# Three other sequences of matmuls for the first feed-forward weight, one per segment

## The reference

```
h = rmsnorm(x, g_mlp[l])
u = jnp.square(jax.nn.relu(jnp.einsum('bsd,df->bsf', h, w_ff1[l])))     # 2048 -> 8192
x = x + jnp.einsum('bsf,fd->bsd', u, w_ff2[l])                          # 8192 -> 2048
```

## Time and profile before

| | |
|---|---|
| median of 3 runs | 2403.76 us (2403.4 to 2403.99) |
| the profiled execution | 2401.66 us, of which the span from first to last instruction is 2399.9 us |
| PE busy | 2392.3 us (100%), 12653 matmuls |
| PEld busy | 2048.4 us (85%), 12653 weight loads |
| DVE busy | 1515.0 us (63%) |
| ACT busy | 1168.0 us (49%) |
| DMA | 452.13 MB, mean 188 GB/s, queue 1 at 58.7% |
| granted TensorE clock | 1.00 over the whole span |

### The profile page before, as it was taken

One profiled execution on the slowest core, in us unless ns is written; L12 is line 12 of the kernel. 1 busy time (PEld: TensorE's weight loads), 2 busy tenths in 40 slices (PEclk: granted clock), 3 DMA queues, 4 the chain that ended last, 5 costly groups with the idle time before them and its releaser, 6 DMA issues.

```text
span 2399.9 us, 30366 instructions
## 1 busy us (share of the span) xinstructions
PE 2392.3 (100%) x12653; PEld 2048.4 (85%) x12653; DVE 1515.0 (63%) x1536; ACT 1168.0 (49%) x1353; POOL 0.2 (0%) x4
## 2 busy tenths in 40 slices
PE   9999999999999999999999999999999999999999
PEld 8788888888888888888888888888888888888887
DVE  6575656666566466566556667855777577756774
ACT  5454454455444344344344555555555455535552
POOL 0000000000000000000000000000000000000000
PEclk9999999999999999999999999999999999999999
DMA  7556556565556665665655565555565665566564
GB/s 251 160 178 197 165 189 196 193 188 197 186 177 203 194 220 193 194 191 190 194 188 182 188 186 164 167 183 185 185 185 196 189 192 177 202 193 187 181 208 143
DMA packets 238037, 452.13 MB, mean 188 GB/s; under 512 B 16569, under 2 KB 20779, under 8 KB 237771
## 3 DMA queue, kind: packets, MB, share of 16 engines
q1 hardware_dynamic: 237147, 449.07, 58.7%
q10 hardware_dynamic: 752, 1.12, 0.1%
HBM read 446.46 MB, written 3.67 MB: 188 GB/s over the span
## 4 chain that ended last, share of the span: by engine, by line
PE 99%; DVE 1%; ACT 0%; DMA 0%; issue 0%; ACTq 0%; DVEq 0%
PE PS L71 99%; DVE WL L71 0%; DMA VR<-in_g_mix 0%; DVE PB L71 0%; DVE TA L71 0%; ACT TA L71 0%; ACT WH L71 0%; DVE SEL L71 0%; DVE NC L71 0%; ACT XHL L71 0%; DVE XHL L71 0%; DVE XT L71 0%; DVE CR L71 0%; DVE SQ L71 0%; ACT CR L71 0%
## 5 line engine op out<-in xcount | busy, mean ns | idle before, releaser
L71 DVE TENSOR_TENSOR WL<-RAW,WH 128x1024 fp32r<-128x1024 f32 (+1 forms) x844 | 1021.9, 1221 | 745.9 <-ACT WH L71 745.6
L71 ACT ACTIVATE WH<-RAW 128x1024 fp32r<-128x1024 f32 (+1 forms) x845 | 881.6, 1054 | 901.7 <-PE PS L71 885.9
L71 PE MATMUL PS<-XHL,WH 128*128 128x512 f32 x3984 | 1252.9, 396 | 1.8 <-DVE CR L71 1.3
L71 PEld LDWEIGHTS PS<-XHL,WL 128*128 128x128 f32 x3968 | 745.4, 188 | 176.1
L71 PE MATMUL PS<-XHL,WL 128*128 128x256 f32 x3968 | 779.6, 278 | 0.0
L71 PE MATMUL PS<-WH,MHL 128*128 128x512 f32 x2240 | 694.1, 390 | 0.0
L71 PEld LDWEIGHTS PS<-XHL,WH 128*128 128x128 f32 x3984 | 606.5, 188 | 6.1 <-DVE CR L71 1.5
L71 PEld LDWEIGHTS PS<-WH,MHL 128*128 128x128 f32 x2240 | 420.4, 188 | 87.1
L71 PE MATMUL PS<-WL,MHL 128*128 128x512 f32 x1120 | 435.8, 389 | 0.0
L71 PEld LDWEIGHTS PS<-WL,MHL 128*128 128x128 f32 x1120 | 210.3, 188 | 42.9
L71 DVE TENSOR_TENSOR TA<-TA,PS 128x1024 f32<-128x1024 f32 x72 | 87.9, 1221 | 9.0 <-ACT TA L71 1.8
(11 more groups left out here) (129 smaller groups left out, 785.9 us busy)
## 6 DMA issues: line engine op xcount, KB each, us to landing
RAW<-in_w_ff SPq DMA_DIRECT2D x256, 512.0 KB, 3.7
RAW<-in_w_in SPq DMA_DIRECT2D x224, 512.0 KB, 3.9
RAW<-in_w_up SPq DMA_DIRECT2D x176, 512.0 KB, 4.0
RAW<-in_w_down SPq DMA_DIRECT2D x88, 512.0 KB, 4.3
RAW<-in_w_mix_out SPq DMA_DIRECT2D x32, 512.0 KB, 3.9
RAW<-in_w_out SPq DMA_DIRECT2D x32, 512.0 KB, 3.7
RAW<-in_w_conv_out SPq DMA_DIRECT2D x16, 512.0 KB, 3.7
RAW<-in_w_attn_out SPq DMA_DIRECT2D x16, 512.0 KB, 4.4
```

Of the source, the lines that this page charges most:

```text
L71: ins = step[1](*step[2], **step[3])
```

## The change

Each segment of w_ff1 is given a name for its sequence: "bank" for segment 0, "short" for segment 1, "one" for segment 2, "two" for segment 3. "two" is the sequence of before, and stays for all other feature items.

- "bank": within a unit, bank by bank: h of both chunks, l of both chunks, then the next bank. The shapes are the same, and so is their order by shape (h, h, l, l); what differs is which bank and which weight block each goes to.
- "one": for each chunk and bank h and then l.
- "short": no matmul of 512 columns. For each chunk and bank three of 256 columns, all onto columns 0:256 of the bank: WH against the high piece, WH against the low piece, WL against the high piece. The bank's right half isn't used, so `fold` becomes a single copy by ACT.

In all feature items, those that keep "two" as well, the waits for both chunks of a unit now stand ahead of the unit's first matmul, where each chunk's wait stood ahead of that chunk's matmuls.

```diff
+FF1_ORDER = ("bank", "short", "one", "two")
...
-                for k, kc in enumerate(kcs):
+                for kc in kcs:
                     PE.wait([need(kc, tok)])
-                    st = first and k == 0
-                    en = last and k == len(kcs) - 1
-                    for j0 in range(0, len(banks), 2):
-                        two = list(enumerate(banks))[j0:j0 + 2]
-                        for j, bank in two:
-                            PE.do(mm, PS[:, b + bank, :], h[:, k, j * P:(j + 1) * P], src[:, kc, :],
-                                  start=st, stop=False, inc=False)
-                        for j, bank in two:
-                            end = j == len(banks) - 1 and k == len(kcs) - 1
-                            t = PE.do(mm, PS[:, b + bank, 0:T], l[:, k, j * P:(j + 1) * P], src[:, kc, 0:T],
-                                      start=False, stop=en, inc=end)
+                nb, nk = len(banks), len(kcs)
+                if order == "two":
+                    work = [(k, j, w, 0, m) for k in range(nk) for j0 in range(0, nb, 2)
+                            for w, m in (("h", 2 * T), ("l", T)) for j in range(j0, min(j0 + 2, nb))]
+                elif order == "bank":
+                    work = [(k, j, w, 0, m) for j in range(nb) for w, m in (("h", 2 * T), ("l", T)) for k in range(nk)]
+                elif order == "one":
+                    work = [(k, j, w, 0, m) for k in range(nk) for j in range(nb) for w, m in (("h", 2 * T), ("l", T))]
+                else:
+                    work = [(k, j, w, c, T) for k in range(nk) for j in range(nb)
+                            for w, c in (("h", 0), ("h", T), ("l", 0))]
+                begun = set()
+                for i, (k, j, w, c, m) in enumerate(work):
+                    start = first and j not in begun
+                    begun.add(j)
+                    stop = last and all(x[1] != j for x in work[i + 1:])
+                    t = PE.do(mm, PS[:, b + banks[j], 0:m], (h if w == "h" else l)[:, k, j * P:(j + 1) * P],
+                              src[:, kcs[k], c:c + m], start=start, stop=stop, inc=i == len(work) - 1)
...
-            a = A.step(nc.scalar.copy, TA[:], PS[:, b:b + 4, T:2 * T], after=[t, evac_done[0]])
-            v = V.step(tt, TA[:], TA[:], PS[:, b:b + 4, 0:T], add, after=[a])
+            if whole:
+                v = A.step(nc.scalar.copy, TA[:], PS[:, b:b + 4, 0:T], after=[t, evac_done[0]])
+            else:
+                a = A.step(nc.scalar.copy, TA[:], PS[:, b:b + 4, T:2 * T], after=[t, evac_done[0]])
+                v = V.step(tt, TA[:], TA[:], PS[:, b:b + 4, 0:T], add, after=[a])
```

More of the change, by code:

```diff
@@ L334, in take, with feature_item @@
             return s, b
-        def feature_item(parts, src, tok, mid=(), small=False, ahead=AHEAD):
+        def feature_item(parts, src, tok, mid=(), small=False, ahead=AHEAD, order="two"):
             s, b = side() if small else take()
@@ L365, in feature_item @@
                 flush()
-            return s, b, t
+            return (s, b, t, True) if order == "short" else (s, b, t)
         def f_item():
@@ L423, in token_item, with fold @@
             return s, b, done if tail else t
-        def fold(s, b, t):
-            a = A.step(nc.scalar.copy, TA[:], PS[:, b:b + 4, T:2 * T], after=[t, evac_done[0]])
-            v = V.step(tt, TA[:], TA[:], PS[:, b:b + 4, 0:T], add, after=[a])
+        def fold(s, b, t, whole=False):
+            if whole:
[3 more added lines that the diff above has]
+                v = V.step(tt, TA[:], TA[:], PS[:, b:b + 4, 0:T], add, after=[a])
             free[s] = [v]
@@ L987, in build @@
                 mid = {2: [lambda: turn_x_item(3, G_MLP, xtok)], 4: [lambda: norm_columns("r2", "sum")]} if seg == 0 and g == 0 else {}
-                it = feature_item(wide(io["w_ff1"][0], 0, ALLK, 2048 * seg + 512 * g), XHL, xtok, mid)
+                it = feature_item(wide(io["w_ff1"][0], 0, ALLK, 2048 * seg + 512 * g), XHL, xtok, mid,
+                                  order=FF1_ORDER[seg])
                 later(ff_evac(it, g, "r2", utok, seg == 0 and g == 0))
```

## The result

| | before | after |
|---|---|---|
| median of 20 runs each | 2402.38 us (2401.71 to 2403.99) | 2406.80 us (2406.51 to 2408.36) |
| ratio after to before | | 1.0019, 95% interval 1.0012 to 1.0026 |
| span of the profiled execution | 2399.9 us | 2405.0 us |
| matmuls | 12653 | 12909 |

What follows compares the result with a forecast made beforehand. PE, busy throughout, was taken as the bound, so time sums distances between matmul starts. Terms 3.0 + 0 + 0 + 0.4 = +3.4 us gave 2405.1 us profiled, 2407.2 us for the median; 8-in-10 range 2402.0 to 2411.5 us.

Steps and rivals of the forecast that it cites:

- "short", +3.0 us: w_ff1 segment 1: 120 ns per short matmul, a triple of 360 ns, 11.7 more than a pair, 256 times.
- The first reading: Segment 1: fixed 16.5 ns per matmul plus 0.411 ns a column, same in both item kinds; triple 364.8 ns, +4.2 us.
- The second reading: Segment 1: h costs f_item's 231.7 ns, leaving l 116.6 ns; triple 349.8 ns, +0.4 us.
- "one", 0: w_ff1 segment 2: same 256 h and 256 l as before, alternating, so no change in time.
- Rival 2: Segments 0 to 2: each successor in the same bank costs 5.0 ns more; +9.2 us in all, 2413.0 us; chance 0.13.
- "bank", 0: w_ff1 segment 0: same 256 h and 256 l, shapes following each other as before, so no change in time.
- Loads keep up: Segment 1: weight loads recorded with 188 ns overlap, transposes' loads stand 109 ns apart, so one every 120 ns fits.
- Fold and units' splitting, 0: Segment 1: DVE loses four additions of 1.22 us off the chain; ACT's copies and idle room leave PE unaffected: 0.
- Hoisted wait, +0.4 us: Program's first unit: PE waits for both chunks' low pieces before its first matmul, +0.4 us, once.
- Rival 1: Segment 1: cost goes by columns, not matmuls; triple 345 to 350 ns, whole change -0.4 to +0.8 us; chance 0.24.
- rival 4: Segment 1: weight loads too slow for an unbroken run of short matmuls; +55 us, 2459 us; chance 0.03.
- Rival 3: Pace at an item's start kept in "bank" and "one", triple 345 ns: -2.2 us, 2401.6 us; chance 0.10.

Runs made afterwards that it cites:

- tensors: Changed kernel with w_ff1 segment 2 alternating weights WH and WL, 512 columns for both: segment 116.06 us, 453.4 ns a pair.
- lag: Changed kernel with w_ff1 segment 1 alternating h and l, each l following the h of another bank and weight block: 90.23 us, 352.5 ns a pair.
- hoist_only: Changed kernel with all four w_ff1 segments back in sequence "two", hoisted waits kept: ratio to before 1.0001 (0.9992 to 1.0010).
- sizes: Changed kernel with w_ff1 segment 0 alternating 512 and 256 columns, both with weights from WH: segment 90.22 us.
- short_only: Changed kernel with only segment 1 in "short", the other segments in "two", hoisted waits kept: ratio to before 1.0012 (1.0003 to 1.0021).
- entry_two: Kernel before, with each feature item's first unit in "two" and its seven others in "one", waits as before: ratio 0.9985, median 2398.42 against 2402.11 us.
- all_one: Kernel before, with every feature item in "one", waits as before: ratio 1.0035 (1.0023 to 1.0048), median 2411.14 against 2403.45 us.
- entry_mid: As entry_two, with the unit behind small matmuls queued in the middle of an item also in "two": ratio to before 0.9984 (0.9975 to 0.9993).
- lead_unit: Every unit of every feature item starts h, h, l, l over two banks, then alternates h, l: ratio to before 1.0022 (1.0013 to 1.0031).

## Why the prediction was right, and where it wasn't

The forecast was 2407.2 us and +3.4; measured are 2406.8 and, by the medians of 20 runs, +4.4. That the absolute time agrees to 0.4 us is luck: the median of before, over more runs, came out 1.4 us below the one the forecast stood on, and that nearly cancels the 1.28 us of segment 2 that the forecast lacked. One of the forecast's own signs of being wrong, "if segment 0 or 2 changes by over 1 us", did show. By its steps:

- **"short", +3.0 us: right.** Measured +2.98; 92.15 us / 768 = 120.0 ns a matmul, flat. The choice of 120 between 115 and 121.6 was right, but the reasons were only half so, and the exact hit is in part luck. The runs of one size give the price directly: 226.7 - 120.0 = 106.7 ns for 256 more columns, 0.417 ns each, which is one cycle of the 2.4 GHz level, and 13.3 ns that don't depend on the size. That the slope comes out at one cycle a column speaks for this split; a third size was not run. And f_item, also a run of one size but with 16 weight columns, pays 5 ns more (231.7 ns) for a reason that no run looked for. The first reading failed because it took a mixed sequence for the sum of its parts: a pair should cost 226.7 + 120.0 = 346.7 and costs 348.3 in "two". The second reading, from f_item, put a triple at 349.8 ns; it is 360.0, and "tensors" shows that XHL as moving operand costs 226.7, not 231.7.
- **"one", 0: wrong.** It cost +1.28 us, a quarter of what the trace lost. The step that failed is "nothing is added", which counted instructions by shape and took their distances for a property of each. The pace depends on the sequence and on how it is entered. Rival 2 would have put +1.3 us here for another reason, the same bank; "bank" with its 0.0 and "lag" with +1.07 refute that reason, although segment 2 lasted 90.44 us, just what rival 2 had named for it.
- **"bank", 0: right**, 90.48 against 90.49.
- **Loads keep up: right**, though PEld shows 100% busy. A recorded load of 188 ns is no bound on the distance between loads, which was 120 ns for 768 in a row. The Trainium skill's "Perfetto Trace Analysis", section "Identifying the Most-Contended Engine", judges TensorE's headroom by that share, together with MFU, the share of the peak rate that the matmuls reach. By the share alone, segment 1 had no headroom left. The trace shows that the share says little about the pace here: in the token items it is 83% (69.55 of 84.00 us, 930 to 1014 us of before), and the 13.3 ns beyond the columns are the same. This and the transposes' loads, 109 ns apart, speak against the loads as the limit at 120.0 ns; no run tried it by itself.
- **Fold and units' splitting, 0: right.** DVE lost its four additions and no segment shows it.
- **Hoisted wait, +0.4 us: right**, 0.39 by the traces, nine of which agree. The first product started at 9.23 us and not at the 8.9 forecast, because DVE's pieces came 0.38 us late in that execution. By time alone it isn't shown: the lowest runs of hoist_only and before are 0.6 us apart, and the interval of the ratio includes 1.
- Rival 1 (cost by columns) and rival 4 (slow loads) fall with 120.0 ns. Rival 3 falls for "bank" and "one", which did not keep the pace of an item's start. Segments can run below "two", at 88.75 us, but by another sequence; that the two have to do with each other isn't shown.

## What to carry to other kernels

On an engine that is never idle, price a reordering by the distance between starts over long stretches of that very sequence; shapes and counts don't give it. Where matmuls of two sizes mix, the same sequence can settle into paces 2% apart, and one different unit at the entry may pick the better one. How long the entry is counts too: 16 matmuls of it worked here, four made in every unit cost 5 us. Put several variants into the segments of one kernel: the same sequence at the same place came out equal to 0.01 us from trace to trace, while whole runs scatter by 2 us. But look at what stands ahead of each: a sequence's pace in one segment holds for that entry.

## What the runs showed of the hardware

- **Two rhythms of one sequence.** h and l alternating: 353.3 or 346.7 ns a pair, each kept over hundreds of matmuls, and turned from slow to fast by eight transposes in two places. Behind a token item "one" starts slow; a whole unit of "two" at the entry gives the fast rhythm, four matmuls h, h, l, l don't. The faster one equals the sum of the pure runs (226.7 + 120.0). "sizes" and "tensors" show that the mixed sizes matter here and the weight tensors don't. What in the engine keeps the phase is open.
- **A short fall of the clock.** Of short_only's +5.6 us in span, 1.6 arise in the 32 matmuls from 89.67 us on, in code that the edit does not touch: they take 7.24 us, where they take 5.67 in before and in the changed kernel. The granted clock there, of short_only and of the changed kernel (columns as above):

```profile
80.00:89.00 9.00, 8.39 (x42) 6.70 (x40) 4.41 (x12) 5.67 (x9) 0.00 (x0) 1.00 0.35 104
90.40:93.40 3.00, 3.00 (x12) 2.61 (x11) 0.77 (x1) 0.66 (x2) 0.00 (x0) 0.50 0.79 245
94.00:100.00 6.00, 6.00 (x37) 5.24 (x36) 2.45 (x2) 2.16 (x3) 0.00 (x0) 1.00 0.33 112
```
```profile
90.40:93.40 3.00, 3.00 (x18) 2.62 (x17) 0.49 (x1) 1.24 (x2) 0.00 (x0) 1.00 0.74 218
```

In the first, PE runs at the lower level (0.50, 1.2 GHz) for these 3 us and gets 12 matmuls done instead of 18. Ahead of it PE had waited 1.3 us at most and was busy 8.39 of 9.00 us; the same wait of 1.3 us stands in traces without the fall (before). Nothing in the code sets these executions apart. Four of the twelve traces have the fall, for instance entry_two:

```profile
90.40:93.00 2.60, 2.60 (x10) 2.21 (x9) 0.11 (x1) 0.00 (x1) 0.00 (x0) 0.50 0.75 248
```

In these four (short_only, all_one, entry_two, entry_mid) the same 32 matmuls take 7.24 to 7.28 us, in the other eight 5.67 to 5.70. So the fall costs 1.6 us. It explains the two groups of executions (before: near 2401.9 and 2403.5): the four traces with it are of the upper group of their kernel, and before, after, hoist_only and lead_unit, without it, of the lower. Wherever an execution's mean granted clock was read as 0.999 and not as 1.000, its time is in the upper group. What brings the fall about in some executions and not in others is open.
